# Root mean squares with tokens on partitions, spread back by TensorE into PSUM, and a fused mask, scale and maximum in the sparse attention

## The reference

```python
def rms_norm(x, g):                       # over the 1024 features of a token
    return x * rsqrt(mean(x * x, -1) + 1e-6) * g

# first block, two layers: x += 0.5 * ffn(rms_norm(x)); x += mixer(rms_norm(x));
#                          x += 0.5 * ffn(rms_norm(x)); x = rms_norm(x)
# second block, two layers, with six vectors per layer from mod = silu(c) @ mod_w[i] + mod_b[i]:
for i in range(2):
    h = rms_norm(x, norm_mix_pre[i]) * (1.0 + sc_m) + sh_m
    y = mixer_ab(h, ...) if i % 2 == 0 else mixer_c(h, ...)
    x = x + (1.0 + g_m) * rms_norm(y, norm_mix_post[i])
    h = rms_norm(x, norm_ffn_pre[i]) * (1.0 + sc_f) + sh_f
    x = x + (1.0 + g_f) * rms_norm(conv_ffn(h, ...), norm_ffn_post[i])

# sparse attention inside mixer_ab: 16 heads, per head and query row a causal softmax over two branches
ss = where(causal, q_rot @ k_slc.T * scale, NEG); p_s = softmax(ss)
sw = where(causal, q_rot @ k_win.T * scale, NEG); p_w = softmax(sw)
```

## Time and profile before

| | |
|---|---|
| median of 3 runs | 2648.35 us (2647.55 to 2649.43) |
| the profiled execution | 2644.78 us, its span 2643.0 us |
| PE busy | 2454.2 us, 93% of the span |
| PE weight loads | 2328.4 us, 88% |
| DVE busy | 1715.0 us, 65% |
| ACT busy | 1190.6 us, 45% |
| mean granted TensorE clock | 0.907 of full speed |

### The profile page before, as it was taken

The page is one execution under the profiler, slowest core; times in us unless marked ns, Lnnn a source line. Parts: engine busy times, 40 slices in busy tenths (PEclk is TensorE's granted clock), DMA queues, the critical chain, the costliest instruction groups (busy, mean ns, idle before and its releaser), DMA issues.

```text
span 2643.0 us, 46370 instructions
## 1 busy us (share of the span) xinstructions
PE 2454.2 (93%) x18418; PEld 2328.4 (88%) x18418; DVE 1715.0 (65%) x2679; ACT 1190.6 (45%) x1720; POOL 50.8 (2%) x100
## 2 busy tenths in 40 slices
PE   7999999989997999998999999898699799897997
PEld 7998978988996999987889899698677799797997
DVE  5557999665554555799855555475643566666766
ACT  5444543354443444443253444345233456444654
POOL 0000000000001000000000000100000000000000
PEclk9999996799998999998599999897655899998999
DMA  6556541255556555654054655543200255353552
GB/s 246 183 182 220 164 173 63 94 186 201 182 182 207 191 183 192 205 175 150 1 179 159 204 183 183 183 160 96 96 1 0 82 189 183 135 160 104 191 181 97
DMA packets 110417, 405.85 MB, mean 154 GB/s; under 512 B 12256, under 2 KB 12384, under 8 KB 109920
## 3 DMA queue, kind: packets, MB, share of 16 engines
q1 hardware_dynamic: 96192, 352.33, 39.8%
q0 software_dynamic: 13824, 50.34, 5.5%
q10 hardware_dynamic: 288, 1.57, 0.2%
HBM read 403.14 MB, written 1.05 MB: 153 GB/s over the span
## 4 chain that ended last, share of the span: by engine, by line
PE 81%; DVE 14%; DMA 2%; ACT 2%; issue 1%; POOL 0%; DVEq 0%; SPq 0%; ACTq 0%
PE bank L479 79%; DVE w_lo L1309 3%; PE bank L617 2%; DVE arena L1469 2%; DMA mod_w_buf<-mod_w 2%; DVE arena L1517 1%; DVE arena L1522 1%; DVE arena L1520 1%; DVE work L1378 0%; DVE arena L1720 0%; DVE rinv L1343 0%; DVE arena L1528 0%; DVE arena L1526 0%; DVE arena L1530 0%; DVE work L1346 0%
## 5 line engine op out<-in xcount | busy, mean ns | idle before, releaser
L479 PE MATMUL bank<-h_hi,w_hi 128*128 128x256 f32 (+1 forms) x4016 | 1166.9, 291 | 58.8 <-DVE w_lo L1309 19.0
L479 PE MATMUL bank<-h_hi,w_lo 128*128 128x256 f32 (+1 forms) x4016 | 1151.1, 288 | 0.0
L1309 DVE TENSOR_TENSOR w_lo<-w_raw,w_hi 128x1024 fp32r<-128x1024 f32 x663 | 806.1, 1220 | 488.2 <-ACT w_hi L990 487.9
L479 PE MATMUL bank<-h_lo,w_hi 128*128 128x256 f32 (+1 forms) x4016 | 1122.8, 286 | 0.0
L990 ACT ACTIVATE w_hi<-w_raw 128x1024 fp32r<-128x1024 f32 x663 | 699.7, 1057 | 761.8 <-PE bank L479 756.2
L479 PEld LDWEIGHTS bank<-h_hi,w_hi 128*128 128x128 f32 x4016 | 791.2, 197 | 81.3 <-issue 47.8
L479 PEld LDWEIGHTS bank<-h_hi,w_lo 128*128 128x128 f32 x4016 | 791.3, 197 | 0.0
L479 PEld LDWEIGHTS bank<-h_lo,w_hi 128*128 128x128 f32 x4016 | 772.1, 195 | 4.5 <-issue 4.3
L479 PE MATMUL bank<-hid_hi,w_hi 128*128 128x256 f32 x1056 | 299.2, 283 | 2.3 <-DVE hid_lo L1394 2.3
L479 PE MATMUL bank<-hid_lo,w_hi 128*128 128x256 f32 x1056 | 298.8, 283 | 0.0
L479 PE MATMUL bank<-hid_hi,w_lo 128*128 128x256 f32 x1056 | 298.8, 283 | 0.0
(11 more groups left out here) (204 smaller groups left out, 1882.9 us busy)
## 6 DMA issues: line engine op xcount, KB each, us to landing
w_raw<-weights SPq DMA_DIRECT2D x663, 512.0 KB, 3.3
mod_w_buf<-mod_w POOLq DMA_DIRECT2D x96, 512.0 KB, 5.4
tabs<-shape_tables SPq DMA_DIRECT2D x1, 1748.0 KB, 15.8
work<-v_bias ACTq DMA_DIRECT2D x2, 768.0 KB, 4.9
x<-x_fm SPq DMA_DIRECT2D x1, 1024.0 KB, 4.9
out_fm<-x SPq DMA_DIRECT2D x1, 1024.0 KB, 3.9
vecs<-vectors SPq DMA_DIRECT2D x1, 712.0 KB, 7.5
tabs<-shape_tables SPq DMA_DIRECT2D x1, 65.0 KB, 4.8
```

What stands on the lines that cost most here:

```text
L479: ins = pe.matmul(o, lhs, rhs, start=start, stop=stop, skip_group_check=share)
L1309: v.tensor_tensor(w_lo[:, n % SPLIT, :], w_raw[:, n % RAW, :], w_hi[:, n % SPLIT, :].bitcast(F32), ALU.subtract).then_inc(lo_ready[n % SPL ...
```

## The change

Four edits.

- The mean square is computed with tokens on partitions: the tile of squares is now the stationary operand (two halves of 128 tokens), and one column of `mean_all` moves. Sixteen matmuls of one column replace eight of 256.
- Square root and reciprocal work on 128 x 2 numbers (`root_tok`). Two more matmuls spread them back: `root_tok`, one column repeated over 128, is the stationary operand and `identity` moves, which leaves the reciprocal root of each token on all partitions in bank 6. DVE's scaling reads it there. `final_norm` copies it to `rinv` first.
- PE has to do these two matmuls between the reciprocal and the scaling. So two of the `mod_w` tiles that stood behind `mean_squares` now stand between the sums and the spreading matmuls, and at place 9 `mod_cols` too. `identity` is loaded with the first tables (NORM_TAB grows from 130 to 258 columns).
- In the sparse attention one DVE operation per branch (`tensor_tensor_reduce`, with mask, scale and minimum) replaces one masking operation over both branches and one maximum over both; the signs are turned, and the exponential takes scale -1. PE's next scores and ACT's exponential both wait for the pair.

```diff
-NORM_TAB = P + 2
+NORM_TAB = 2 * P + 2
...
-            def mean_squares():
+            def mean_squares(mods=0, turned=False):
                 for kt in range(KT):
                     pe.wait_ge(sq_ready, w.next(sq_ready))
-                    mm(half(6, 0), tab("mean_all"), work[:, kt, :], kt == 0, kt == KT - 1,
-                       stat_full if kt == KT - 1 else None)
+                    for tt in range(TT):
+                        mm(bank[6][:, SEQ + tt:SEQ + tt + 1], work[:, kt, tt * P:(tt + 1) * P],
+                           tab("mean_all")[:, 0:1], (kt, tt) == (0, 0), kt == KT - 1,
+                           stat_full if (kt, tt) == (KT - 1, TT - 1) else None, share=True)
+                mod_tiles(mods)
+                if turned:
+                    mod_cols()
+                pe.wait_ge(recip_ready, w.next(recip_ready))
+                for tt in range(TT):
+                    mm(half(6, 0)[:, tt * P:(tt + 1) * P], root_tok[:, tt:tt + 1].broadcast_to([P, P]), tab("identity"),
+                       sig=spread_ready if tt == TT - 1 else None)
...
             for l in range(DEPTH):
-                mean_squares()
+                mean_squares(2 if l else 0)
                 if l:
-                    mod_tiles(2)
                     mod_cols()
                     mod_tiles(6)
                 ffn(l > 0)
                 mod_tiles(3)
-                mean_squares()
-                mod_tiles(3)
+                mean_squares(2)
+                mod_tiles(1)
                 first_mixer(l)
...
             for l in range(DEPTH):
-                mean_squares()
+                mean_squares(2 if l == 0 else 0, l == 0)
                 if l == 0:
-                    mod_tiles(2)
-                    mod_cols()
                     mod_tiles(6)
...
-                act_f(rinv[:, :], half(6, 0), ACT.Sqrt, bias=tab("eps")).then_inc(root_ready, 1)
+                act_f(root_tok[:, :], bank[6][:, SEQ:SEQ + TT], ACT.Sqrt, bias=tab("eps")).then_inc(root_ready, 1)
...
             def norm(gain, shift=None):
 
                 dve.wait_ge(root_ready, w.next(root_ready))
-                v.reciprocal(rinv[:, :], rinv[:, :]).then_inc(dve_link, 1)
-                dve.wait_ge(dve_link, w.next(dve_link))
+                v.reciprocal(root_tok[:, :], root_tok[:, :]).then_inc(recip_ready, 1)
+                dve.wait_ge(spread_ready, w.next(spread_ready))
                 for kt in range(KT):
-                    v.scalar_tensor_tensor(work[:, kt, :], x[:, kt, :], gain[:, kt:kt + 1], rinv[:, :],
+                    v.scalar_tensor_tensor(work[:, kt, :], x[:, kt, :], gain[:, kt:kt + 1], half(6, 0),
                                            ALU.mult, ALU.mult).then_inc(scaled, 1)
...
-                    v.scalar_tensor_tensor(s, bank[u % 2][:, 0:2 * length].rearrange("p (b k) -> p b k", b=2), SCALE,
-                                           rows(tab(f"causal{qt}"), 2), ALU.mult, ALU.add).then_inc(sc_free, 1)
-                    dve.wait_ge(sc_free, w.next(sc_free))
-                    v.tensor_reduce(nmax[:, 2 * u:2 * u + 2], s, X_AXIS, ALU.max, negate=True).then_inc(smax, 1)
+                    for br in range(2):
+                        v.tensor_tensor_reduce(s[:, br], bank[u % 2][:, br * length:(br + 1) * length],
+                                               tab(f"causal{qt}"), -SCALE, -4.0 * NEG, ALU.add, ALU.min,
+                                               nmax[:, 2 * u + br:2 * u + br + 1]).then_inc(sc_taken, 1)
```

More of the change, by code:

```diff
@@ L115 @@
 TABLES, N_TAB = {}, 0
-for _name, _width in (("mean_all", P), ("one", 1), ("eps", 1),
-                      ("identity", P), ("mean_head", P), ("rot", P), ("rot16", P),
+for _name, _width in (("mean_all", P), ("one", 1), ("eps", 1), ("identity", P),
+                      ("mean_head", P), ("rot", P), ("rot16", P),
                       ("dup0", P), ("dup1", P), ("rotdup0", P), ("rotdup1", P),
@@ L203, in build @@
         rinv = sb("rinv", SEQ)
+        root_tok = sb("root_tok", TT)
         w_raw = sb("w_raw", RAW, TILE)
@@ L344, in build @@
         stat_full = sem("mean_square_in_psum")
+        recip_ready = sem("reciprocal_root_ready")
+        spread_ready = sem("reciprocal_root_spread_in_psum")
         root_ready = sem("root_ready")
@@ L375, in build @@
         smax = sem("score_maximum_ready")
+        sc_taken = sem("branch_scores_and_maximum_ready")
         p_ready = sem("probabilities_ready")
@@ L882, in scores @@
                     if u >= 2:
-                        pe.wait_ge(sc_free, w.next(sc_free))
+                        pe.wait_ge(sc_taken, w.next(sc_taken, 2))
                     for br in range(2):
@@ L916, in recurrent_nsa_mixer @@
                         values(u - 2)
-                pe.wait_ge(sc_free, w.next(sc_free, 2))
+                pe.wait_ge(sc_taken, w.next(sc_taken, 4))
                 pe.wait_ge(y2_ready, w.next(y2_ready))
@@ L1054, in conv_step, with heads @@
                 act_f(gate_a[:, par, :], gate_a[:, par, :], ACT.Silu).then_inc(gate_ready, 1)
-            def heads(count, exponentials, turned, n_turned):
+            def heads(count, maxima, per, exponentials, turned, n_turned):
                 for u in range(count + 1):
                     if u < count:
-                        act.wait_ge(smax, w.next(smax))
+                        act.wait_ge(maxima, w.next(maxima, per))
                         exponentials(u)
@@ L1107, in exponential @@
                           accum_out=rsum[:, u:u + 1]).then_inc(p_ready, 1)
-                heads(units, exponential, probs_t, lambda u: 4 * P)
+                heads(units, smax, 1, exponential, probs_t, lambda u: 4 * P)
                 for i in range(KT):
@@ L1217, in exponentials @@
                                     s2[:, u % 2, br * length:(br + 1) * length], ACT.Exp, bias=nmax[:, k:k + 1],
-                                    accum_out=rsum[:, k:k + 1])
+                                    scale=-1.0, accum_out=rsum[:, k:k + 1])
                     ins.then_inc(p_ready, 1)
-                heads(nsa_units, exponentials, pt2, lambda u: 2 * (u // NSA_HEADS + 1) * P)
+                heads(nsa_units, sc_taken, 2, exponentials, pt2, lambda u: 2 * (u // NSA_HEADS + 1) * P)
                 for b in range(4):
@@ L1354, in final_norm @@
                 dve.wait_ge(root_ready, w.next(root_ready))
-                v.reciprocal(rinv[:, :], rinv[:, :]).then_inc(dve_link, 1)
+                v.reciprocal(root_tok[:, :], root_tok[:, :]).then_inc(recip_ready, 1)
+                dve.wait_ge(spread_ready, w.next(spread_ready))
+                v.tensor_copy(rinv[:, :], half(6, 0)).then_inc(dve_link, 1)
                 dve.wait_ge(dve_link, w.next(dve_link))
@@ L1374, in add_normed @@
                 dve.wait_ge(root_ready, w.next(root_ready))
-                v.reciprocal(rinv[:, :], rinv[:, :]).then_inc(dve_link, 1)
-                dve.wait_ge(dve_link, w.next(dve_link))
+                v.reciprocal(root_tok[:, :], root_tok[:, :]).then_inc(recip_ready, 1)
+                dve.wait_ge(spread_ready, w.next(spread_ready))
                 for kt in range(KT):
-                    ins = v.scalar_tensor_tensor(work[:, kt, :], y[:, kt, :], gain[:, kt:kt + 1], rinv[:, :],
+                    ins = v.scalar_tensor_tensor(work[:, kt, :], y[:, kt, :], gain[:, kt:kt + 1], half(6, 0),
                                                  ALU.mult, ALU.mult)
```

## The result

The changed kernel took 2661.36 us in the median (2659.25 to 2663.78) where the kernel before took 2647.55: 1.0052 times as long, 95% interval 1.0037 to 1.0066. The profiled execution of the changed kernel has a span of 2659.5 us, 16.5 more than before, at a mean granted clock of 0.894 (0.907 before).

What follows compares the result with a forecast made beforehand. It took PE to bound the kernel, 81% of the span, and asked what PE waits for at the sixteen root mean squares. Terms -7.0 + 16.5 + 8.1 = +17.6 us gave 2666.0 us on the median; 8-in-10 range 2645 to 2677.

Steps and rivals of the forecast that it cites:

- Chain, -7.0: Square root to first scaling: 1.35 us at full clock, 1.75 at half, against 2.3; with earlier-ending sums, -7.0 us together.
- The 1 us for sums that end earlier: Last record of the sums, one column instead of 256, ends about 0.1 us earlier: some 1 us over all places.
- Tiles ahead, +16.5: Places 2 to 9: scaling also waits for `mod_w` tiles put ahead of the spreading, delaying scaling and products: +16.5 us.
- The final norms' 5.5: Places 4 and 8: later scaling, +1.8 and +2.75 us, plus a copy out of PSUM each: +5.5 us in all.
- Sums, +8.1: Sums that start cold, places 1, 5, 11, 13, 15: 32 one-column records take 6.8 us at half clock, +8.1 us.
- nothing at the places that follow dense products: Sums behind dense products: 32 records take about 3.5 us, as before (3.72), so no cost there.
- The reason given: For the sums: records bound by loading their weights let the clock fall and did not raise it, clock 0.50.
- Attention, 0: Sparse attention: two fused DVE operations with reads make 1.0 us, hidden by PE's own work; cost nothing.
- Rival 2: Short sums keep the clock as before, tiles still delay: sum -0.8 us, 2647.5 us; chance 0.20.
- The rule of the Trainium skill: PE gaps throttle the clock, so keep matmuls coming; by it the change keeps the clock as it was or better.
- Rival 3: Tiles do not bind, second tile over by 222.5 at place 2: chain gain 13 us, 2635 us; chance 0.13.
- Rival 4: Sparse attention's fused operation above 0.75 us; with 1.25 us each, +32 us on top, 2698 us; chance 0.05.

Runs made afterwards that it cites:

- experiment 3: Changed kernel with sums over 128 moving columns and the `mod_w` tiles back behind the spreading at places 2 to 8: 2623.63 us, 0.9925 times the kernel before.
- experiment 1: Changed kernel with each sum of squares moving 128 columns of `mean_all` instead of one: 2637.81 us, 0.9976 times the kernel before.
- experiment 7: The kernel of experiment 3 plus 44 unread products while PE waits, at places 1, 8, 10, 12 and 14: 2612.91 us, 0.9879 times the kernel before.

## Why the prediction was right

The sum came to +17.6 us and 2666.0, which is 18.4 over the 2647.55 of the runs here. Measured were +13.8, and on repetition 1.0070, which is +18.5 on 2647.55 (there the two medians on one chip were 21.7 apart). Its direction and both causes hold. Point by point:

- **Chain, -7.0:** gained too little. The prices at both clocks were near (1.35 and 1.75 predicted, 1.26 in experiment 3 and 1.78 in the changed kernel measured), but at places 10, 12, 14 and 16 the forecast took full clock because dense products stand ahead. The sums themselves bring the clock down before the spreading, so the gain there was 0.53 each instead of 0.95: -2.1 for -3.8. Places 1, 11, 13 and 15 gave -2.1 for -2.2. The 1 us for sums that end earlier didn't come: at place 2 their records take 3.73 us for 3.72, and the square root starts 3.77 us after the first of them for 3.76.
- **Tiles ahead, +16.5:** right in mechanism, near in size. The scaling came later by 2.4 at places 2 and 3 (up to 2.6 predicted for place 2), 1.65 at place 4 and 2.2 at place 8 with their copies (2.2 and 3.2 predicted), 0.9 at place 5 (1.0) and 1.0 at place 9 (0.8). Places 2 and 3 were over-priced in the products: the first product came 1.3 us later at place 2 (1.6 predicted) and 0.8 later at place 3, and at place 2 the clock was back at 1.00 after some 1.5 us of products instead of 4, so by the prediction's own price some 0.7 us was lost there and not 1.8. At places 6 and 7, counted from the square root, the scaling came 2.0 and 1.6 us later and the first product 0.6 later and 1.0 earlier (1.2 later predicted for each). Undoing this part gave 12 us. The final norms' 5.5 adds up to 5.4.
- **Sums, +8.1:** the most under-sized term, 13.3. (With the 6.8 us that the text gives, its five places make 7.6; eight records in 0.95 us make 3.8 for 32 and not 3.5, which leaves the zero as it is.) Place 11, 13, 15 and 1 came out as said (7.0 each, +1.9, +1.8, +0.5, +1.1). Place 9, which had no term here, gave +0.6. Place 5 took 4.9 in this trace and 7.0 in the second one (6.8 predicted). Not foreseen: sums that start at full clock behind dense products lose it on the way, at places 4, 6, 7, 8, 10, 14 and 16, 6.2 us together. The step "nothing at the places that follow dense products" failed. The reason given was too wide as well: not every record that is bound by its weight load lets the clock fall. The sums of 128 columns take 0.120 us a record beside 0.117, with PEld as busy, and the clock rises during them in experiment 1.
- **Attention, 0:** right. The fused operation takes 0.29 us in the 16 units of 128 keys (under the 0.35 assumed) and 0.42 in the 16 units of 256 (over it), its read 0.08 (0.15 assumed). The operations of a unit thus sum to 0.74 and 1.01 us, against 0.84 and 1.38 before. Turns of units start at 1955.02, 1957.53 and 1960.05, 2.51 us apart, as before.
- **Rival 2** (the short sums keep the clock) is what experiment 1 built, and it isn't what the change does. The rule of the Trainium skill cited in the prediction ("TensorE: Matmul & The Clock Gate", "HAM oscillation — how this bites in real kernels") is borne out by half. Keeping products of 256 columns coming did hold the clock through the sums of place 11 in experiment 7 (1.00, where it was 0.65 over the same sums in experiment 3), but at place 10 of the changed kernel records that came without a gap and moved one column did not (1.00, then 0.50). **Rival 3** is out: the second tile ended at 224.45 at place 2, not by 222.5. **Rival 4** is out by the 0.29 and 0.42, with 0.08 for the read.

That the total was so close is in part luck. On the profiled executions the sums were forecast 5 us too low and the rest 6 too high. Sums and chains together grew by 23.3 us, and the 7 us that brought this down to 16.5 were in no term: for the most part they lie where the trace of the kernel before happened to be slow.

## What to carry to other kernels

Before you turn a matmul round so that it moves one column, count the clock: the clock fell under such records here although PE read as fully busy, and widening the moving side cost 0.1 us a place and gave 20 us in all. When a short step of the critical chain moves onto an engine that also has side work in its queue, put it ahead of that work: behind two tiles, spreading matmuls of 0.7 to 1.2 us cost 12 us over seven places. A change can hold a gain (16 to 19 us here) and still come out slower, so price its parts apart before you drop it.

## What the runs showed of the hardware

- In the sums every record loads 128x128 float32 weights. With 1 moving column a record takes 0.117 us at full clock and 0.218 at half (3.73 / 32 and 6.99 / 32), with 128 columns 0.120 at full clock (3.84 / 32). At full speed 127 more columns cost 0.003 us a record; what differs is the clock.
- At the program's start the clock's column misleads. In the changed kernel it reads 1.00 at place 1, while PE runs at the pace that it has at half clock, 11 records in 2 us as at place 11:

```profile
8.00:10.00 2.00, 2.00 (x11) 2.00 (x11) 0.00 (x0) 1.98 (x4) 0.00 (x0) 1.00 1.01 410
10.00:12.00 2.00, 2.00 (x11) 2.00 (x11) 0.00 (x0) 0.12 (x1) 0.00 (x0) 1.00 1.05 426
```

- A reciprocal of 128 x 2 numbers takes 0.17 us, of 128 x 8 0.19, of 128 x 256 1.75. With tokens on partitions, 2 columns hold what took 256 before, and that layout is the cheap one for it.
